# A trunk of four hybrid layers on one core: one mask product per head, the setup and tables of the state-space layer reordered, and x transposed in parts at three block borders

## What is computed

```python
for i in range(4):
    mixer = (stick_breaking, s5, latent, stick_breaking)[i]
    channel = (dense_swiglu, moe_swiglu)[i % 2]     # even layers dense, odd layers experts
    x = x + mixer(rms_norm(x))
    x = x + channel(rms_norm(x))
return rms_norm(x)

# stick breaking, 16 heads of 64
z = q @ k.T / 8
strict = key < query
log_one_minus = where(strict, log_sigmoid(-z), 0)
tail = sum of log_one_minus over the later keys
out = where(strict, exp(log_sigmoid(z) + tail), 0) @ v

# dense SwiGLU, 2816 wide
out = (silu(h @ w_gate) * (h @ w_up)) @ w_down
```

## Time and profile before

| what | value |
|---|---|
| runs | 1732.41, 1736.39, 1738.27 us; median 1736.39 |
| the profiled execution: time, and its span | 1734.57 us, 1732.9 us |
| TensorE matmul busy | 1668.0 us (96% of the span) |
| VectorE busy | 1293.6 us (75%) |
| ScalarE busy | 1002.6 us (58%) |
| GpSimd busy | 220.3 us (13%) |
| TensorE's mean granted clock | 0.990 of full |
| read from and written to HBM | 426.63 and 21.10 MB, 258 GB/s over the span |

### The profile page before, as it was taken

How to read it: one execution, slowest core, us unless ns; L and a number is a source line. 1 busy time by engine, 2 the same in 40 slices (tenths; PEclk the granted TensorE clock), 3 DMA queues, 4 the chain that set the end, 5 groups by cost and what they waited for, 6 DMA issues and landing times.

```text
span 1732.9 us, 26753 instructions
## 1 busy us (share of the span) xinstructions
PE 1668.0 (96%) x11011; PEld 1545.0 (89%) x11011; DVE 1293.6 (75%) x1283; ACT 1002.6 (58%) x920; POOL 220.3 (13%) x230
## 2 busy tenths in 40 slices
PE   6999999989999999999989999999999999999996
PEld 6999999779899999999779999998998999999995
DVE  4578998785789888888867555446548888888886
ACT  5565333343576777777645443335557777777773
POOL 4407992010000000000210000000000000000011
PEclk9999999989999999999999999999999999999998
DMA  7427887575389899999942254454334999999993
GB/s 287 144 110 261 266 307 247 205 281 189 140 326 375 342 370 358 374 354 359 363 150 106 74 218 182 146 186 168 113 142 180 364 353 349 373 349 368 358 383 150
DMA packets 53482, 449.28 MB, mean 259 GB/s; under 512 B 6736, under 2 KB 8944, under 8 KB 16640
## 3 DMA queue, kind: packets, MB, share of 16 engines
q1 hardware_dynamic: 48480, 430.40, 66.0%
q0 software_dynamic: 4896, 17.35, 2.8%
HBM read 426.63 MB, written 21.10 MB: 258 GB/s over the span
## 4 chain that ended last, share of the span: by engine, by line
PE 73%; DVE 12%; ACT 6%; issue 4%; DMA 3%; POOL 1%; POOLq 0%; DVEq 0%; ACTq 0%; SPq 0%
PE PS L323 21%; PE PS L325 21%; PE PS L324 21%; DVE wlo L375 5%; ACT whi L368 3%; DMA yg<-expert_rows,offi 1%; DMA expert_rows<-ysb 1%; PE PS L2084 1%; PE PS L2047 1%; PE PS L2048 1%; PE PS L1722 1%; PE PS L495 1%; PE PS L896 1%; DVE x L2314 1%; DMA raw<-in_weights 1%
## 5 line engine op out<-in xcount | busy, mean ns | idle before, releaser
L375 DVE TENSOR_TENSOR wlo<-raw,whi 128x3072 fp32r<-128x3072 f32 (+1 forms) x278 | 854.9, 3078 | 186.7 <-ACT whi L368 185.8
L368 ACT ACTIVATE whi<-raw 128x3072 fp32r<-128x3072 f32 (+1 forms) x278 | 705.9, 2541 | 330.1 <-PE PS L325 305.0
L323 PE MATMUL PS<-wlo,hT_hi 128*128 128x384 f32 (+3 forms) x1840 | 594.2, 323 | 1.9 <-DVE wlo L375 1.4
L325 PE MATMUL PS<-whi,hT_hi 128*128 128x384 f32 (+3 forms) x1840 | 591.0, 321 | 0.0
L324 PE MATMUL PS<-whi,hT_lo 128*128 128x384 f32 (+3 forms) x1840 | 591.0, 321 | 0.0
L323 PEld LDWEIGHTS PS<-wlo,hT_hi 128*128 128x128 f32 x1840 | 347.2, 189 | 6.1 <-DVE wlo L375 1.7
L324 PEld LDWEIGHTS PS<-whi,hT_lo 128*128 128x128 f32 x1840 | 347.3, 189 | 2.9
L325 PEld LDWEIGHTS PS<-whi,hT_hi 128*128 128x128 f32 x1840 | 347.1, 189 | 0.3
L323 PE MATMUL PS<-wlo,mhi 128*128 128x512 f32 x352 | 143.5, 408 | 0.8 <-DVE mlo L2338 0.8
L324 PE MATMUL PS<-whi,mlo 128*128 128x512 f32 x352 | 139.1, 395 | 0.0
L325 PE MATMUL PS<-whi,mhi 128*128 128x512 f32 x352 | 139.1, 395 | 0.0
(11 more groups left out here) (394 smaller groups left out, 2051.1 us busy)
## 6 DMA issues: line engine op xcount, KB each, us to landing
raw<-in_weights SPq DMA_DIRECT2D x203, 1536.0 KB, 8.1
raw<-in_weights SPq DMA_DIRECT2D x73, 1024.0 KB, 7.1
raw<-s_tables SPq DMA_DIRECT2D x8, 1536.0 KB, 7.2
expert_rows<-ysb POOLq DMA_DIRECT2D x14, 512.0 KB, 9.6
s_tables<-g_out SPq DMA_DIRECT2D x8, 640.0 KB, 3.5
t_af<-s_rows_af SPq DMA_DIRECT2D x32, 128.0 KB, 3.8
s_tables<-g_out SPq DMA_DIRECT2D x8, 512.0 KB, 3.7
raw<-in_weights SPq DMA_DIRECT2D x3, 1152.0 KB, 11.1
```

What stands on the lines that cost most here:

```text
L323: pe.matmul(o, sh, mlw, start=start, stop=False, skip_group_check=True)
L325: return pe.matmul(o, sh, mh, start=False, stop=stop, skip_group_check=True)
L368: act.activation(whi[p0 % SPL][:, 0:n], raw[p0 % RAW][:, 0:n], ACT.Copy).then_inc(hi_done, 1)
L375: dve.tensor_tensor(wlo[p0 % SPL][:, 0:n], raw[p0 % RAW][:, 0:n], whi[p0 % SPL][:, 0:n].bitcast(F32), ALU.subtract).then_inc(lo_done, 1)
```

## The change

Three edits that share no data:

1. **Mask.** `tri_r` becomes 128 x 256, the triangle twice. One product per head writes both diagonal blocks, its output columns being 0 to 127 and 256 to 383 of the bank. So 32 pairs of products of 128 columns become 32 products of 256.
2. **Setup and tables of S5.** `s5_setup_act2` moves from ahead of the attention block to between the splits of its fourth and fifth weight piece. On VectorE, powers 0 go ahead of the first split of the dense block, and taps 0 right behind it, where powers 0 were; taps 1 to 3 and powers 1 to 3 keep their places.
3. **x in parts.** At the three borders chunks 0 to 3 are turned as soon as the first columns of x are complete (`x_early`, set by VectorE): half way through tile (2, 1) at the first two borders, before the last quarter of the last down product at the third. Chunks 4 and 5 follow the last tile, 6 and 7 come by `late_turns` ahead of k = 4 of the first gate product; at the third border 4 to 7 come behind the first third of the first key block. `hT_lo` on VectorE is split to match (`hT_low`), a weight split goes between chunks 5 and 6 of norms 1 and 5, and `CHUNK_AT` has the order of banks that this needs.

The diff, cut: the narrower pad ahead of the wider constant, the slices `tri_r[:, 0:P]` in `tails` and the argument `n` at calls are left out.

```diff
-                    ("big_r", [P, P], F32R), ("tri_r", [P, P], F32R), ("one_r", [P, P], F32R))
+                    ("big_r", [P, P], F32R), ("tri_r", [P, 2 * P], F32R), ("one_r", [P, P], F32R))
...
-        AFTER_PROJ = ((6, 0), (7, 0), (2, 0), (3, 0), (4, 0), (5, 0), (6, 1), (7, 1))
+        EARLY = {1: 1, 5: 2, 6: 3}
         CHUNK_AT = {0: ((0, 0), (1, 0), (2, 0), (3, 0), (7, 0), (4, 0), (5, 0), (6, 0)),
-                    1: AFTER_PROJ, 5: AFTER_PROJ,
+                    1: ((6, 0), (7, 0), (2, 0), (4, 0), (6, 1), (7, 1), (3, 0), (5, 0)),
+                    5: ((6, 0), (7, 0), (2, 0), (3, 0), (6, 1), (7, 1), (4, 0), (5, 0)),
                     4: ((4, 0), (5, 0), (6, 0), (7, 0), (2, 0), (3, 0), (4, 1), (5, 1)),
                     6: ((0, 0), (1, 0), (2, 0), (3, 0), (0, 1), (1, 1), (2, 1), (3, 1))}
...
+        def hT_low(dve, n, ks):
+            for k in ks:
+                dve.wait_ge(nrm_hi, HI0[n] + k + 1)
+                dve.scalar_tensor_tensor(out=hT_lo[:, k, :], in0=chunk(n, k), scalar=gain_of(n, k),
+                                         in1=hT_hi[:, k, :].bitcast(F32), op0=ALU.mult, op1=ALU.subtract)\
+                    .then_inc(nrm_lo, 1)
...
             if n not in WHOLE:
-                for k in range(KC):
-                    dve.wait_ge(nrm_hi, HI0[n] + k + 1)
-                    dve.scalar_tensor_tensor(out=hT_lo[:, k, :], in0=chunk(n, k), scalar=gain_of(n, k),
-                                             in1=hT_hi[:, k, :].bitcast(F32), op0=ALU.mult, op1=ALU.subtract)\
-                        .then_inc(nrm_lo, 1)
+                if n in (1, 5):
+                    hT_low(dve, n, (4, 5))
+                    split_lo(dve, base[STAGES[n]] + SPL - 2)
+                    hT_low(dve, n, (6, 7))
+                    mean_sq(dve, n)
+                    split_lo(dve, base[STAGES[n]] + SPL - 1)
+                    return
+                hT_low(dve, n, range(4 if n == 6 else 0, KC))
...
-            turn_x(pe, n, range(KC))
+            turn_x(pe, n, range(4, KC) if n == 6 else (6, 7))
...
+                        if (i, t) == (2, 1) and k == KC // 2:
+                            pe.wait_ge(x_early, EARLY[n])
+                            turn_x(pe, n, range(4))
...
-
-        def proj_dve(dve, b0, banks):
+            turn_x(pe, n, (4, 5))
...
+        def proj_dve(dve, b0, banks, n):
             for i, (c0, w) in enumerate(DCOLS):
                 dve.wait_ge(w_used, b0 + i + 1)
                 for t in range(TT):
                     ins = dve.tensor_tensor(x[:, t, c0:c0 + w], x[:, t, c0:c0 + w], PS[:, banks[i][t], 0:w], ALU.add)
                     if i == len(DCOLS) - 1:
                         ins.then_inc(x_up, 1)
-                if i < len(DCOLS) - 2:
-                    split_lo(dve, b0 + i + SPL)
+                if i == 0:
+                    split_lo(dve, b0 + SPL)
+                elif i == 1:
+                    ins.then_inc(x_early, 1)
+                    hT_low(dve, n, range(4))
...
                 piece_ready(pe, p)
+                hT_ready(pe, norm, 3)
+                part(0, range(4))
                 late_turns(pe, norm)
-                hT_ready(pe, norm, 3)
-                for c in range(3):
+                for c in range(1, 3):
                     part(c, range(4))
...
-                    pe.matmul(z[:, 0:P], big_r[:], tri_r[:], start=False, stop=False, skip_group_check=True)
-                    last = pe.matmul(z[:, L:L + P], big_r[:], tri_r[:], start=False, stop=False, skip_group_check=True)
+                    last = pe.matmul(z.rearrange("p (a q) -> p a q", a=2)[:, :, 0:P], big_r[:],
+                                     tri_r[:].rearrange("p (a q) -> p a q", a=2), start=False, stop=False,
+                                     skip_group_check=True)
...
-                    if a == 1 and (i, t) == (2, 1) and k == KC // 2:
-                        pe.wait_ge(x_most, 2)
-                        turn_x(pe, 7, range(6))
+                    if (i, t) == (2, 1) and k == KC // 2:
+                        if a == 0:
+                            pe.wait_ge(x_early, EARLY[1])
+                            turn_x(pe, 1, range(4))
+                        else:
+                            pe.wait_ge(x_most, 2)
+                            turn_x(pe, 7, range(6))
...
                 pe.wait_ge(at_w, 8)
                 out_tile(2, 1, range(KC)).then_inc(w_used, 1)
+                turn_x(pe, 1, (4, 5))
...
             split_hi(act, b0 + 3)
-            split_hi(act, b0 + 4)
             if a == 0:
                 act.wait_ge(cst2_in, 16)
+                s5_setup_act2(act)
+            split_hi(act, b0 + 4)
             act.activation(big_r[:], ident, ACT.Copy, scale=BIG).then_inc(at_cm, 1)
-            act.activation(tri_r[:], negtri, ACT.Copy).then_inc(at_cm, 1)
+            act.activation(tri_r[:].rearrange("p (a q) -> p a q", a=2),
+                           negtri.rearrange("p (a q) -> p a q", a=1).to_broadcast([P, 2, P]), ACT.Copy).then_inc(at_cm, 1)
...
                     if by_chunk and t == 0:
-                        if k == 0:
+                        if k == 4:
                             late_turns(pe, n)
                         hT_ready(pe, n, k)
...
                 for t in range(TT):
+                    if (f, i, half, t) == (1, JD - 1, 1, 1):
+                        pe.wait_ge(x_early, EARLY[6])
+                        turn_x(pe, 6, range(4))
...
             for j in range(JD):
-                if f == 0 and j >= 1:
+                if f == 0 and j == 0:
+                    s5_powers_dve(dve, 0)
+                if f == 0 and j >= 2:
                     s5_taps_dve(dve, j - 1)
                 if j >= 1:
                     low_part(j - 1)
                 split_lo(dve, b0 + ND["g", j] + SPL)
                 if f == 0:
-                    s5_powers_dve(dve, j)
+                    (s5_powers_dve if j else s5_taps_dve)(dve, j)
                 if j >= 2:
                     split_lo(dve, b0 + ND["d", j - 2] + SPL)
...
                     if half == 1:
                         i.then_inc(x_up, 1)
+                if f == 1 and half == 0:
+                    i.then_inc(x_early, 1)
+                    hT_low(dve, 6, range(4))
...
             s5_setup_act(act)
-            s5_setup_act2(act)
             sb_act(act, 0, 0)
```

More of the change, by code:

```diff
@@ L307, in hybrid_trunk @@
         gain_in = sem("gain_in")
-        x_up, x_most, p_half = sem("x_up"), sem("x_most"), sem("p_half")
+        x_up, x_most, p_half, x_early = sem("x_up"), sem("x_most"), sem("p_half"), sem("x_early")
         first_hi, first_lo = sem("first_hi"), sem("first_lo")
@@ L895, in tails @@
                     for part in (SL[i % 2], AH[i % 2]):
[L896 removed]
+                        pe.matmul(z[:, 0:384], tri_r[:, 0:P], part[:, j, 0:384], start=False, stop=False,
                                   skip_group_check=True)
```

7 lines of the change are left out of this document (3 added, 4 removed).

## The result

The changed kernel takes 1739.57 us (median of 20 runs, 1736.38 to 1742.87), the kernel before 1734.36 (20 runs, 1730.73 to 1740.81). The ratio is 1.0025 with a 95% interval of 1.0016 to 1.0034: +4.3 us, between 2.8 and 5.9; the medians differ by 5.2. The profiled execution of the change has a span of 1735.1 at a mean granted clock of 0.988, against 1732.9 and 0.990 before, so the traces alone show +2.2. With its 1736.63 us that execution is the second fastest of its twenty, so the two traces show less than the runs.

What follows compares the result with a forecast made beforehand. TensorE, 73% of the chain of waits, was taken as the bound. Terms -2.4 - 0.3 + 4.0 - 1.2 + 2.9 = +3.0 on 1734.57 gave 1737.6 us, range 1729 to 1743, judged no change.

Steps and rivals of the forecast that it cites:

- mask product: Scores of both attention blocks: 32 merged products save 0.11 us each, partly taken by waits; -2.4 us, ends 0 and -3.5.
- setup: Program start: GpSimd stops beside VectorE's moved split, so the first softplus starts little earlier; -0.3 us, ends -2.7 and +0.5.
- first border and tables: Attention to first dense block: VectorE's splits and tables come late and TensorE waits; +4.0 us, ends +1.5 and -4.
- second border: Latent attention to dense: VectorE is free, no wait, 0.9 us of idle time goes; -1.2 us, ends -1.4 and -0.6.
- third border: Dense to second attention: later low part adds 1.3 us, low clock 1.6; +2.9 us, ends -0.5 and +3.0.
- The sign that was to show it: Scores: 32 mask products of 256 columns, 0.11 us apart, would show the mask forecast right.
- The reading by which time goes by columns alone: Mask products: 134 cycles for 128 columns, 262 for 256, so merging saves nothing and the sum is 2.4 us higher.
- The rival with two stretches of output: Mask products: one with two stretches of output takes 0.22 us, the 2.4 are lost; 1740.0 us, chance 0.08.
- The wait for L1401: First dense block near 173: TensorE waits 4.4 us for the product of gate and up, plus 1.6 at low clock.
- Fillers: Rival: GpSimd not stopped, mask saves 3.0 us, first border's product in time; -8.6 us, 1726.0, chance 0.25.
- VectorE behind: Rival: the first table step's lag reaches the second, another wait and low clock; +5.1 us on the forecast, 1742.7, chance 0.17.
- the low clock goes: First dense block: the wait of 1.9 us at 191.65 goes and with it about 1.6 us of low clock.

Runs made afterwards that it cites:

- setup: The kernel before with only the S5 table setup on ScalarE moved between the splits of the fourth and fifth weight piece; ratio 0.9994.
- mask_contig: The kernel before with merged mask products, each writing columns 0 to 255 in one stretch (wrong values); 1730.97 us in one execution.
- setup_late: The kernel before with the S5 table setup on ScalarE behind both splits and the three attention constants; 1735.79 us in one execution.
- mask: The kernel before with only the mask products merged, 256 columns in two stretches of output; ratio 0.9995, 1733.45 us.

## Why the prediction was right or wrong, point by point

The sign and the "within 0.3%" came out, and nearly the +3.0 on the profiled execution: +2.2 between the traces, +0.25% in the runs, 1739.57 inside the range of 1729 to 1743. The terms:

| term | forecast | measured in the trace | from |
|---|---|---|---|
| mask product | -2.4 | -0.8 in the first block, -1.4 in D | all six kernels with the edit |
| setup | -0.3 | -0.7 | setup, from the landing of x |
| first border and tables | +4.0 | +4.65 against that trace, +5.75 against the mean | A |
| second border | -1.2 | -1.5 | B |
| third border | +2.9 | +2.8, of it 1.35 the wait | C |

Against the one trace of before these sum to +3.0, the forecast. Read from the change itself, the first block is 1.6 shorter from the landing of x on, then come +4.65, -1.5, +2.8 and -1.45; what is left of the span, with the same code in both, is 0.7 shorter by the clock and the landing of x. That gives the +2.2.

**Mask.** The price of 0.22 a call was right, and so were the places where a wait takes it (0.9 and 1.5 forecast, 0.8 and 1.4 measured). The sign that was to show it was not: the mask products themselves give only 0.16 a call, and the two of a call start 0.22 apart and not 0.11; the rest comes from the weight product behind them. The reading by which time goes by columns alone, and nothing is saved, fell too. The rival with two stretches of output fell with `mask_contig`; the Trainium skill, "PSUM — Partial Sum Buffer", section "Specifications (TRN2)", had spoken for it, and no run here shows such a slowing.

**Setup.** Right in each step: GpSimd stops for 3.51 us and ends at 35.1 (35.7 forecast). The stop beside a split was the reason to give this edit little; it gained 0.7. That the wait for keys, which it removes, is often followed by the low clock was not seen, as the trace of before has none there; `setup_late` shows what such a stretch can cost, 3.0. The Trainium skill, "SBUF — State Buffer", section "SBUF: two separate sides", says that a VectorE instruction with two inputs in SBUF and a GpSimd instruction that reads SBUF exclude each other for the whole instruction; the rows agree, with 0.5 us operations that take 3.4 to 3.75 beside a split of some 3.5.

**First border and tables.** The wait in the last tile was forecast at 2.8 and is 2.71; none is left near 192. The wait for L1401 was forecast at 4.4 and is 5.98: of the terms, powers 0 took 6.1 (159.99 to 166.09) and not 5.4, taps 0 6.75 and not 6.4, the split at 156.13 3.94. TensorE was 0.9 later at the place, as forecast (1.0). The sum of the steps up to L1401 is 177.8, not 177.9, which changes nothing. The low clock behind the wait cost 1.25, not 1.6: TensorE took 18.74 us from one transposition to the next (177.50 to 196.24) where it took 17.49 with full clock (172.31 to 189.80, its arrival before the wait of 1.85).

**The rivals.** Fillers fell with the wait of 5.98. VectorE behind did not go on to the second table step: the product at 196.24 is not waited for. Its support was misread: the digits of GpSimd are 7 for the slice from 130 to 173 and 9 only from 173 to 260. What I had not listed is what each part does alone: the tables gain 1.2, and the border costs 4.3 of the 5.75.

**What was weak, and what was luck.** The weak step was not a term but the ground of the sum: the profiled execution of before had the low clock at both places, 1.1 us more than the mean of seven traces of the same code. So its terms "the low clock goes" were charged as certain, where it comes only in some executions. And 1739.4, the forecast set on the three runs, lies 0.2 from the measured 1739.57 by luck in part: those three had a median 2.0 above that of all twenty, and the difference came out 1.3 (by the ratio) to 2.2 us (by the medians) above +3.0.

## What to carry to other kernels

Before an engine is given work earlier, list what stands behind it on the engine that has to finish it: here VectorE's list, not TensorE's, set the price, and an edit that gained 1.2 alone met one that cost 4.3 alone in a wait of 6 us. Test the parts alone and in pairs, then keep those whose stretch of the trace gets shorter; that gave the one version here whose interval lies below the kernel before. A sum made against one profiled execution inherits its clock; take a few traces of unchanged code first, to see which stretches scatter. And count a lead from an instruction that both traces share, not from the start: the landing of x moved by up to 1.4 us, twice what the setup edit gained.

## What the runs showed of the hardware that was not expected

- The low clock (1.2 GHz) behind a wait of 1 to 2.6 us is a matter of the execution: at 144 and 192 it came in the trace of before (0.57, 0.58) and in neither place in that of `mask` (1.00), with waits of 2.1 and about 2 in both. At the third border a wait of 2.50 was followed by it in two traces of three. What a stretch with it costs depends on the place: 0.8 at 144, 1.35 at 192, 1.4 at the third border, 1.5 in B and 3.0 behind the wait of 2.60 in `setup_late`.
- In front of the first scores waits of 2.05, 2.16 and 2.57 us for the keys were not followed by it, and seven of 2.7 to 3.5 were.
- Even with short waits (1.1 us at 965.57), stretch B took 94.2 in the seven traces with neither edit nor low clock, 92.7 in the three with the edit, 95.7 in the two with the low clock, and 94.2 in the two with both. Two effects of 1.5 us with opposite sign can so hide each other in one trace.
- Over 101 executions of the kernel before, time and mean granted clock go together with a correlation of -0.70: 0.001 of clock is 1.0 us. The executions of the change had a mean clock of 0.986, those of before 0.988. By that slope some 2.4 of the 4.3 us, as an estimate, go together with the clock.
- Operations of GpSimd on 128 x 1 or 32 x 128 elements take 3.4 to 3.75 us beside a split of VectorE and 0.5 to 0.6 elsewhere.
- Four mask products take 0.50 us: the first, behind the scores, 0.17, the others 0.11. Two of 256 columns take 0.34, 0.22 and 0.12, and the weight product behind them gets 0.05 to 0.06 shorter.
